# A two-block state space, MLP and gated recurrence kernel: input rows between half weight blocks, decays by a broadcast transfer, output in token halves

## The chip, the cores and the metric

The kernel runs on one core of one Trainium2 chip. The metric is the device time of one execution in microseconds (us). The core has a tensor engine (PE, matmul), a vector engine (DVE), a scalar engine (ACT), GpSimd (POOL) and SyncE (SP), which here only issues transfers. All share one on-chip memory; matmuls accumulate in eight banks of 128 x 512 float32. Transfers run on 16 DMA engines.

## The reference, cut to what matters

Activations are 512 tokens of 1024 channels, float32. Two layers follow each other.

```python
# first layer
u = rmsnorm(x, norm_mix_w)
proj = u @ w_in                       # gate_a, gate_s, b, c, v, z, xbc, dt
y_a = (b * causal_dwconv(c * v, conv_a_w)) @ w_a_out
dt = softplus(dt_raw + dt_bias); a = -exp(a_log)
a_cum = cumsum(dt * a)                # within chunks of 128 tokens
chunk_decay = exp(a_cum[..., -1])     # (4 chunks, 32 heads)
carry = carry * chunk_decay + states  # from chunk to chunk
h = x + (sigmoid(gate_a) * y_a + sigmoid(gate_s) * y_s) @ w_o
h = h + conv_gated_mlp(rmsnorm(h, norm_ffn_w))
h = rmsnorm(h, final_norm_w)
# second layer: gated recurrence (8 heads, both directions) and spatial gating
h = h + merged @ w_out_2
out = rmsnorm(h, final_norm_w_2)
```

## The kernel before

Everything is held transposed, channels on the partitions: `X[128, 8, 512]` is eight rows of 128 channels by 512 tokens. All weights are cut into 285 blocks of 1024 x 128, 512 KB each, in one list `STREAM`. For each block SyncE loads `raw` (ring of four), ACT copies it rounded to `w_high` (ring of three), DVE subtracts to get `w_low`, and PE runs 24 matmuls of 512 columns: for each of eight k `w_high` x high part, `w_high` x low part, `w_low` x high part of the moving activation, all into one bank. The copies of a block are made two blocks ahead of its matmuls (`ahead`). The order on every engine is written out by hand; semaphores tie the engines together (`landed`, `hi_done`, `lo_done`, `block_done`).

The start. SyncE issues the parameters `par`, block 0, X rows 0 to 3 in two transfers, block 1, rows 4 to 7 in two transfers, the constants `cst`, block 2, block 3, and from then on one block for every block done. PE runs four dummy matmuls on `conv_p`, memory set to 1.0. ACT makes `w_high` of block 0, the high part of rows 0 and 1 (`first_row`: X times the norm weight into `early_high`), `w_high` of block 1, rows 2 to 7, block 2, then the squares of all rows (`first_square`). DVE makes the low parts in the same order (`low_row`, `low`), then the sums of squares. The norm's root is applied later, since the first blocks are multiplied before it is known. PE's `pair_blocks` runs blocks 0 and 1 (`conv_c`, `conv_v` of channel block 0) together, with the second `lead=3` steps behind the first; a step's first matmul waits until the row's low part is there (`s_split`). The third block is `conv_b`. Then `stat(0)` sums the squares over the partitions, ACT takes the root, and DVE and ACT make the rows with the root (`u_high`, `u_low`), which PE uses from the seventh block on.

The decays of chunks. After the 25th block (`dt`) DVE and ACT work out `dtw` (32 heads by 512 tokens) and the four decays of each head. DVE multiplies them with an identity (`dsmall[:, 1]`); PE, after the `gate_a` blocks, transposes `dtw` (L608) and multiplies ones with that product (L610), so that every partition has all 128 decays, and DVE copies both out (L1531, L1532). They are used in the state recurrence, `states`. GpSimd's queue writes the running sums to memory and reads them back, one head at a time, to all partitions (`rows_of`, L2072); ACT takes their exponential (L997).

The end. The last block is run in two token halves of 256 (`last_block`): 24 matmuls for each half. `last_stat(half)` sums the squares of a half over the partitions; that of half 0 stands inside half 1's matmuls, ahead of k = 6. ACT takes the root (L1378, L1379). DVE adds the last row (`last_row`, L2047) and scales (L2054) eight rows of half 0, with half 1's `last_row` behind the first, then eight rows of half 1. SyncE stores two rows of all 512 tokens whenever two rows of half 1 are scaled:

```python
for k in range(0, KT, 2):
    sp.wait_ge(s_fin, k + 2)
    sp.dma_start(out.rearrange("(k p) t -> p k t", p=P)[:, k:k + 2], X2[:, k:k + 2]).then_inc(s_out, 16)
```

Of the kernel before, what the change touches and what calls it, by code (L numbers as in the profile page):

```python
# [14 lines left out]
P = 128  # L15
T = 512
# [3 lines left out]
HEADS = 32  # L20
# [210 lines left out]
def build(nc, x_in, wall, par_in, consts_in, masks_in, ws_in, bs_in, spill, running, out):  # L231
    ctx = ExitStack()
    with ctx:
# [29 lines left out]
        identR = fixed("identR", [P, P], F32R)  # L263
# [3 lines left out]
        decay_b = fixed("decay_b", [P, NCH, HEADS], F32)  # L267
# [126 lines left out]
        s_x = [sem(f"s_x{k}") for k in range(KT // 2)]  # L394
# [12 lines left out]
        s_min, s_exp, s_mat, s_y, s_ytaken = (sem(f"ssd_{k}") for k in "min exp mat y ytaken".split())  # L407
        s_rows, s_row = sem("ssd_rows"), [sem(f"ssd_row{k}") for k in range(4)]
# [63 lines left out]
        def _(sp):  # L472
            def load_x(k):
                sp.dma_start(X[:, k:k + 2], x_in.rearrange("(k p) t -> p k t", p=P)[:, k:k + 2]).then_inc(s_x[k // 2], 16)

            sp.dma_start(par[:], par_in).then_inc(s_par, 16)
            for n in range(NBLK):
# [3 lines left out]
                if n == 0:  # L481
                    load_x(0)
                    load_x(2)
                if n == 1:
                    for k in range(4, KT, 2):
                        load_x(k)
                    sp.dma_start(cst[:], consts_in).then_inc(s_cst, 16)
                if n == 2 * RAW_RING:
# [4 lines left out]
            sp.wait_ge(s_out, KT // 2 * 16)  # L493

        @block.tensor
        def _(pe):
# [22 lines left out]
            def pair_blocks(first, second, moving, ready, base, stop=True, between=None, lead=0):  # L519
# [4 lines left out]
                for step in range(KT + lead):  # L524
                    for key, k in ((first, step), (second, step - lead)):
                        if not 0 <= k < KT:
                            continue
# [11 lines left out]
                    if between and step == KT // 2 + 1:  # L539
                        between()  # L540

# [8 lines left out]
            def last_block():  # L550
# [54 lines left out]
            for j in range(3):  # L605
                for c in range(NCH):
                    k = j * NCH + c
                    pe.transpose(side[0][:, k * HEADS:(k + 1) * HEADS], dtw[:, j, c * P:(c + 1) * P],  # L608
                                 cst[0:HEADS, 0, 0:HEADS])
            pe.matmul(side[1][:, 0:NCH * HEADS], cst[0:HEADS, 1], dsmall[:, 1],  # L610
                      start=True, stop=True).then_inc(d_turned, 1)
# [230 lines left out]
        def _(act):  # L842
# [47 lines left out]
            def first_row(k):  # L890
                act.wait_ge(s_x[k // 2], 16)
# [490 lines left out]
        def _(dve):  # L1382
# [62 lines left out]
            dve.wait_ge(s_par, 16)  # L1445
# [31 lines left out]
            for k in range(KT):  # L1477
                mixed_row(k)
                if k in (3, 6):
                    low(5 + (3, 6).index(k))  # L1480
            link(tt(w_both[:], par[:, PCOL["final_norm_w"]:PCOL["final_norm_w"] + KT],
                    par[:, PCOL["norm_w_2"]:PCOL["norm_w_2"] + KT], ALU.mult))
            for j in range(KT):
# [17 lines left out]
                if j == LATE:  # L1501
                    link(cp(identR[:], ident))
# [678 lines left out]
```

## Time and profile before

| | |
|---|---|
| median of 3 runs | 1728.76 us (1727.35 to 1729.48) |
| profiled execution | 1729.27 us |
| its span, first to last instruction | 1727.4 us |
| PE busy | 1707.5 us, 99% of the span |
| PE weight loads (beside the matmuls) | 1401.7 us |
| DVE busy | 1149.6 us, 67% |
| ACT busy | 815.3 us, 47% |
| granted TensorE clock, mean | 0.997 of full |
| moved by the DMA | 174.75 MB, mean 101 GB/s |

All rows come from one profiled execution; its time is 1.87 us more than its span. Times in rows are counted from the span's start. L followed by a number is a line of the kernel; a line can be that of a helper. "Idle before" is how long the engine stood still ahead of an instruction, with what released it.

### The profile page before, as it was taken

The page shows a single profiled execution, that of the slowest core. Times are in us where ns is not written, and L with a number is a line of the kernel's source. Part 1 is how long each engine was busy: PE and PEld are TensorE (multiplying, and loading weights), DVE is VectorE, ACT ScalarE, POOL GpSimd, SP SyncE. Part 2 cuts the span into 40 slices and gives each one's busy share as a digit, 9 for nine tenths or more (in the row PEclk, how much of TensorE's full clock was granted, in tenths as well). Part 3 has the DMA queues.
Part 4 walks back from the last instruction along what each step waited for, and adds up shares of the span by engine and source line. Part 5 has one row for each costly group of instructions (what it writes and reads, how often), then busy time and mean ns, then how long its engine had stood idle before and what let it go on. Part 6 is the DMA issues. An engine that isn't in the chain of part 4 may idle for free.

```text
span 1727.4 us, 22168 instructions
## 1 busy us (share of the span) xinstructions
PE 1707.5 (99%) x8794; PEld 1401.7 (81%) x8794; DVE 1149.6 (67%) x1686; ACT 815.3 (47%) x1162; POOL 29.7 (2%) x55
## 2 busy tenths in 40 slices
PE   8999999999999999999999999999999999999997
PEld 6888888878877888888888888888888888888886
DVE  6844346888886645677775445867768778867664
ACT  5323234755756323322222334667667676665521
POOL 0000000000000000000000000100000000000000
PEclk9999999999999999999999999999999999999999
DMA  4333323333332222223323333722222222222422
GB/s 158 129 98 124 98 98 98 110 105 103 113 107 86 89 96 97 97 98 98 98 98 98 110 101 107 256 86 74 86 74 75 85 74 78 82 86 74 135 96 75
DMA packets 48934, 174.75 MB, mean 101 GB/s; under 512 B 5552, under 2 KB 5680, under 8 KB 48704
## 3 DMA queue, kind: packets, MB, share of 16 engines
q1 hardware_dynamic: 43648, 155.45, 27.4%
q0 software_dynamic: 5184, 17.89, 3.3%
q8 instruction: 70, 1.15, 0.3%
q14 instruction: 32, 0.26, 0.1%
HBM read 164.87 MB, written 4.26 MB: 98 GB/s over the span
## 4 chain that ended last, share of the span: by engine, by line
PE 96%; DVE 2%; ACT 1%; DMA 0%; issue 0%; SPq 0%; DVEq 0%; ACTq 0%
PE bank L513 84%; PE bank L535 2%; PE bank L740 2%; PE bank L668 1%; PE bank L578 1%; PE bank L750 1%; PE bank L666 1%; PE bank L626 1%; PE bank L786 0%; DMA raw<-stream 0%; PE bank L775 0%; PE bank L763 0%; PE bank L647 0%; DVE w_low L1391 0%; DVE X L2054 0%
## 5 line engine op out<-in xcount | busy, mean ns | idle before, releaser
L513 PE MATMUL bank<-u_high,w_high 128*128 128x512 f32 x1568 | 618.4, 394 | 0.0
L513 PE MATMUL bank<-u_high,w_low 128*128 128x512 f32 x1568 | 610.9, 390 | 0.0
L513 PE MATMUL bank<-u_low,w_high 128*128 128x512 f32 x1568 | 610.0, 389 | 0.0
L851 ACT ACTIVATE w_high<-raw 128x1024 fp32r<-128x1024 f32 x285 | 301.0, 1056 | 587.3 <-PE bank L513 579.6
L1391 DVE TENSOR_TENSOR w_low<-raw,w_high 128x1024 fp32r<-128x1024 f32 x285 | 348.2, 1223 | 250.0 <-ACT w_high L851 244.5
L513 PEld LDWEIGHTS bank<-u_high,w_low 128*128 128x128 f32 x1568 | 294.3, 188 | 62.0
L513 PEld LDWEIGHTS bank<-u_high,w_high 128*128 128x128 f32 x1568 | 294.4, 188 | 61.8 <-issue 2.9
L513 PEld LDWEIGHTS bank<-u_low,w_high 128*128 128x128 f32 x1568 | 294.6, 188 | 60.6 <-issue 1.2
L1471 DVE TENSOR_TENSOR h_raw<-bank,rs 128x512 f32<-128x512 f32 x44 | 30.4, 691 | 62.2 <-PE bank L513 55.4
L513 PE MATMUL bank<-f_high,w_high 128*128 128x512 f32 x176 | 68.5, 389 | 0.0
L513 PE MATMUL bank<-f_low,w_high 128*128 128x512 f32 x176 | 68.5, 389 | 0.0
L513 PE MATMUL bank<-f_high,w_low 128*128 128x512 f32 x176 | 68.5, 389 | 0.0
L1833 DVE TENSOR_TENSOR XL<-AG 128x512 f32<-128x512 f32 x80 | 51.6, 686 | 22.8 <-PE bank L740 22.8
L1195 ACT ACTIVATE XL<-XL 128x512 f32<-128x512 f32 x56 | 35.2, 629 | 62.3 <-DVE XL L1833 42.1
L859 ACT ACTIVATE stage<-bank 128x512 f32<-128x512 f32 x24 | 14.3, 595 | 73.5 <-PE bank L513 64.7
L513 PE MATMUL bank<-y_high,w_high 128*128 128x512 f32 x112 | 43.7, 390 | 0.3 <-DVE w_low L1391 0.3
L513 PE MATMUL bank<-y_high,w_low 128*128 128x512 f32 x112 | 43.6, 389 | 0.0
L513 PE MATMUL bank<-y_low,w_high 128*128 128x512 f32 x112 | 43.6, 389 | 0.0
L1851 DVE TENSOR_TENSOR XL<-XL,Q 128x512 f32<-128x512 f32 x56 | 38.3, 688 | 7.4 <-ACT XL L1196 7.1
L1722 DVE TENSOR_TENSOR X<-X,bank 128x512 f32<-128x512 f32 x23 | 15.8, 688 | 35.9 <-PE bank L513 35.7
L513 PEld LDWEIGHTS bank<-f_high,w_high 128*128 128x128 f32 x176 | 33.0, 188 | 6.9
L513 PEld LDWEIGHTS bank<-f_high,w_low 128*128 128x128 f32 x176 | 33.0, 188 | 6.9
(357 smaller groups left out, 2421.9 us busy)
## 6 DMA issues: line engine op xcount, KB each, us to landing
raw<-stream SPq DMA_DIRECT2D x285, 512.0 KB, 3.3
rows<-running POOLq DMA_DIRECT2D x32, 256.0 KB, 3.5
X<-x_t SPq DMA_DIRECT2D x4, 512.0 KB, 7.9
u_high<-n_high_rows POOLq DMA_DIRECT2D x4, 512.0 KB, 5.7
u_low<-n_low_rows POOLq DMA_DIRECT2D x4, 512.0 KB, 6.4
residual<-X POOLq DMA_DIRECT2D x4, 512.0 KB, 8.8
X<-residual POOLq DMA_DIRECT2D x4, 512.0 KB, 5.4
out_t<-X SPq DMA_DIRECT2D x4, 512.0 KB, 3.6
```

Source lines behind the costliest of these rows:

```text
L513: ins = pe.matmul(acc[:], w[:, k], x[:, at + k], start=start and k == first and j == 0, stop=stop and k == KT - 1 and j == 2)
L535: ins = pe.matmul(bank(key)[:], w[:, k], x[:, k], start=k == 0 and j == 0, stop=stop and k == KT - 1 and j == 2)
L578: ins = pe.transpose(side[2][:, n * P:(n + 1) * P], src[:, c * P:(c + 1) * P], ident)
L626: ins = pe.transpose(bank3[:, c * P:(c + 1) * P], src[:, c * P:(c + 1) * P], ident)
L666: ins = pe.matmul(y[rows, cs], xdec[:, c - 1, hs], cexp[h % 4][:, cs], start=False, stop=True)
L740: ins = pe.matmul(side[at % 2][half * e:half * e + half, to], XL[:, at % 3, 0, keys], XL[:, at % 3, 1, to], start=True, stop=True)
L851: act.activation(w_high[:, n % HI_RING], raw[:, n % RAW_RING], ACT.Copy).then_inc(hi_done, 1)
L1195: act.activation(x[:, 0], x[:, 0], ACT.Exp, scale=1.0 if n == 0 else -1.0)
L1391: tt(w_low[:, n % RAW_RING], raw[:, n % RAW_RING], w_high[:, n % HI_RING].bitcast(F32), ALU.subtract).then_inc(lo_done, 1)
L1471: give(tt(out, bank(key)[:], rs[:], ALU.mult), key)
L1833: ins = tt(two(x, first, step, w), a, b, ALU.subtract)
L1851: tt(x, x, Q[:, h % 2], ALU.mult).then_inc(x_pair, 1)
```

## The change

Start: X comes in eight transfers of one row, and blocks 0 and 1 come in two halves of four k each. The order is half block 0, the first eight columns of the parameters, row 0, half block 1, rows 1 to 3, second half 0, row 4, second half 1, rows 5 to 7, block 2, constants, the other parameters, block 3. ACT and DVE make `w_high` and `w_low` of these blocks by halves. PE runs three dummies instead of four, and a new `first_blocks` runs both blocks side by side, k by k; its first matmul of a row waits for the row's high part alone, the second for the low part. `pair_blocks` loses `lead`, which only this place used.

Middle: the decays are written by GpSimd's queue to memory and read back to all partitions. DVE's product, PE's matmul and DVE's copy go, and so does an unused rounded copy of the identity. `decay_b` is laid out heads by chunks.

End: `last_stat(0)` stands ahead of k = 4. `last_row(1)` stands behind the fourth scaling of half 0. Each scaling counts `s_fin`. Half 0 is stored in two transfers of four rows, half 1 in four transfers of two rows, each of 256 tokens.

```diff
@@ sync
+            def load_half(n, half):
+                ks = slice(half * KT // 2, (half + 1) * KT // 2)
+                sp.dma_start(raw[:, n, ks], wall[n].rearrange("p (k c) -> p k c", k=KT)[:, ks]).then_inc(
+                    landed[n] if half else half_landed[n], 16)
+
+            first_columns = PCOL["norm_mix_w"] + KT
+            load_half(0, 0)
+            sp.dma_start(par[:, 0:first_columns], par_in[:, 0:first_columns]).then_inc(s_norm, 16)
+            load_x(0)
+            load_half(1, 0)
+            for k in range(1, 4):
+                load_x(k)
+            load_half(0, 1)
+            load_x(4)
+            load_half(1, 1)
+            for k in range(5, KT):
+                load_x(k)
+            for n in range(2, NBLK):
...
-            for k in range(0, KT, 2):
-                sp.wait_ge(s_fin, k + 2)
-                sp.dma_start(out.rearrange("(k p) t -> p k t", p=P)[:, k:k + 2], X2[:, k:k + 2]).then_inc(s_out, 16)
+            for half, rows in enumerate((4, 2)):
+                ts_ = slice(half * T // 2, half * T // 2 + T // 2)
+                for k in range(0, KT, rows):
+                    sp.wait_ge(s_fin, half * KT + k + rows)
+                    sp.dma_start(out.rearrange("(k p) t -> p k t", p=P)[:, k:k + rows, ts_], X2[:, k:k + rows, ts_]).then_inc(s_out, 16)
@@ tensor
+            def first_blocks():
+
+                for k in range(KT):
+                    for n in range(2):
+                        if n == 0:
+                            pe.wait_ge(n_high, k + 1)
+                        if k == 0:
+                            pe.wait_ge(hi_half, n + 1)
+                        elif k == KT // 2:
+                            pe.wait_ge(hi_done, n + 1)
+                        pe.matmul(ps[n][:], w_high[:, n, k], early_high[:, k], start=k == 0, stop=False)
+                        if n == 0:
+                            pe.wait_ge(s_split, k + 1)
+                        pe.matmul(ps[n][:], w_high[:, n, k], early_low[:, k], start=False, stop=False)
+                        if k == 0:
+                            pe.wait_ge(lo_half, n + 1)
+                        elif k == KT // 2:
+                            pe.wait_ge(lo_done, n + 1)
+                        ins = pe.matmul(ps[n][:], w_low[:, n, k], early_high[:, k], start=False, stop=k == KT - 1)
...
-                        if half and k == KT - 2:
+                        if half and k == KT // 2:
                             last_stat(0)
...
-            for _ in range(4):
+            for _ in range(3):
                 pe.matmul(side[1][:], conv_p[:, 0:P], conv_p[:], start=True, stop=True)
-            pair_blocks(("conv_c", 0), ("conv_v", 0), EARLY_ROWS, s_split, KT * EARLY, lead=3)
+            first_blocks()
...
-            pe.matmul(side[1][:, 0:NCH * HEADS], cst[0:HEADS, 1], dsmall[:, 1],
-                      start=True, stop=True).then_inc(d_turned, 1)
+            ins.then_inc(d_turned, 1)
@@ scalar
-            high(0)
-            act.wait_ge(s_par, 16)
-            for k in range(2):
+            high_half(0, 0)
+            act.wait_ge(s_norm, 16)
+            first_row(0)
+            high_half(1, 0)
+            for k in range(1, 4):
                 first_row(k)
-            high(1)
-            for k in range(2, KT):
+            high_half(0, 1)
+            first_row(4)
+            high_half(1, 1)
+            for k in range(5, KT):
                 first_row(k)
@@ vector
-            low(0)
+            low_half(0, 0)
+            dve.wait_ge(s_norm, 16)
             for k in range(KT):
                 low_row(EARLY, k, pcol("norm_mix_w", k), *first)
-                if k == 1:
-                    low(1)
+                if k == 0:
+                    low_half(1, 0)
+                if k == 3:
+                    low_half(0, 1)
+                if k == 4:
+                    low_half(1, 1)
...
+            dve.wait_ge(s_par, 16)
...
-                    link(cp(identR[:], ident))
...
-            cp(decay_b[:].rearrange("p c h -> p (c h)"), side[1][:, 0:NCH * HEADS]).then_inc(d_tok, 1)
+            cp(tok[:].rearrange("p a c h -> p (a c h)"), side[0][:, 0:3 * NCH * HEADS]).then_inc(d_tok, 1)
...
+            dve.wait_ge(s_decay, 32)
...
-                    if half == 0 and k == 0:
+                    stt(X2[:, k, ts_], X2[:, k, ts_], pcol("final_norm_w_2", k), rs[:, ts_], ALU.mult, ALU.mult).then_inc(s_fin, 1)
+                    if half == 0 and k == 3:
                         last_row(1, side[2])
@@ gpsimd
+            pool.wait_ge(d_exp, 2)
+            pool.dma_start(decays, dsmall[:, 0, 4:8]).then_inc(s_decay, 16)
             pool.wait_ge(s_rows, 16)
+            pool.wait_ge(s_decay, 16)
+            pool.dma_start(decay_b[:].rearrange("p h c -> p (h c)"),
+                           bass.AP(decays.tensor, decays.offset, [[0, P], [1, NCH * HEADS]])).then_inc(s_decay, 16)
```

## Rows read from the trace of the kernel before

**Rows 1.** From the page: busy time of PE, with its share of the span.
```profile
PE 1707.5 (99%) x8794; PEld 1401.7 (81%) x8794; DVE 1149.6 (67%) x1686; ACT 815.3 (47%) x1162; POOL 29.7 (2%) x55
```

**Rows 2.** The chain that ended last, 0 to 60 us: start, us, what.
```profile
2.64 7.90 DMA raw<-stream
...
13.60 11.43 PE bank L535 x42
25.03 5.44 PE bank L513 x24
```

**Rows 3.** Windows of the start: busy (x), PEclk, DMA share, GB/s.
```profile
0.00:4.00 4.00, 2.04 (x3) 1.01 (x4) 0.72 (x5) 1.28 (x1) 0.20 (x4) 1.00 0.56 174
4.00:5.00 1.00, 1.00 (x3) 0.48 (x2) 0.00 (x0) 0.39 (x1) 0.00 (x0) 1.00 0.76 150
5.00:8.00 3.00, 3.00 (x5) 0.88 (x4) 1.22 (x1) 0.67 (x1) 0.00 (x0) 1.00 1.00 321
8.00:13.00 5.00, 1.75 (x7) 1.00 (x6) 2.76 (x4) 3.77 (x6) 0.00 (x0) 1.00 1.04 409
8.10:9.60 1.50, 0.00 (x0) 0.00 (x0) 0.79 (x2) 1.29 (x2) 0.00 (x0) 1.00 1.03 404
11.30:13.60 2.30, 0.00 (x1) 0.01 (x1) 1.95 (x3) 2.30 (x5) 0.00 (x0) 1.00 1.06 424
13.60:17.10 3.50, 3.50 (x9) 2.72 (x10) 3.50 (x6) 3.50 (x6) 0.00 (x0) 0.52 0.41 166
```

**Rows 4.** Timeline of PE, 0 to 9 us: the dummies.
```profile
1.96 6.14 PE L591 MATMUL bank<-conv_p 128*128 128x512 f32 x8 [1.96 <-DVE conv_p L1418]
```

**Rows 5.** Line L474, the X transfers: issue ns and starts, landing.
```profile
L474 SPq DMA_DIRECT2D X<-x_t x4: 427/494/1430, 1.7 to 3.7; - x4
...
DMA to landing us min/median/max: 6.3/7.9/9.3
```

**Rows 6.** Groups by line and shape, 0 to 31 us: busy us, mean ns.
```profile
L1391 DVE TENSOR_TENSOR w_low<-raw,w_high 128x1024 fp32r<-128x1024 f32 x5 | 6.1, 1225 | 7.8 <-ACT w_high L851 7.8
L1428 DVE SCALAR_TENSOR_TENSOR early_low<-X,par,early_high 128x512 fp32r<-128x512 f32 x8 | 5.5, 748 | 1.8 <-ACT early_high L874 1.8
L851 ACT ACTIVATE w_high<-raw 128x1024 fp32r<-128x1024 f32 x5 | 5.3, 1053 | 3.8 <-DMA raw<-stream 3.8
L874 ACT ACTIVATE early_high<-X,par 128x512 fp32r<-128x512 f32 x8 | 5.1, 708 | 2.4 <-DMA X<-x_t 2.4
L888 ACT ACTIVATE sq_first<-X 128x512 f32<-128x512 f32 x8 | 4.3, 614 | 0.0
L1454 DVE TENSOR_TENSOR sums<-sums,sq_first 128x512 f32<-128x512 f32 x6 | 4.2, 692 | 0.2
```

**Rows 7.** Timeline of DVE, 45 to 47 us.
```profile
45.35 1.47 DVE L1423 TENSOR_TENSOR u_low<-scaled,u_high 128x512 fp32r<-128x512 f32 x2
```

**Rows 8.** The chain, 190 to 200 us.
```profile
195.43 0.30 PE bank L610 x2
```

**Rows 9.** Transfers by line: KB each, median us from issue to landing.
```profile
rows<-running POOLq DMA_DIRECT2D x32, 256.0 KB, 3.5
```

**Rows 10.** Line L997, the exponentials of rows: ns, first and last start.
```profile
L997 ACT ACTIVATE cexp<-rows x32: 613/617/633, 294.1 to 539.9; 128x512 f32<-128x512 f32 x32
```

**Rows 11.** The chain, from 1690 us to the end.
```profile
1708.98 5.03 PE bank L562 x42
...
1715.88 0.48 DVE X L2054
...
1719.07 0.40 DVEq L233
1719.46 3.17 DVE X L2054 x8
```

**Rows 12.** Timeline of ACT, 1717 to 1728 us.
```profile
1718.44 0.42 ACT L1379 ACTIVATE rs<-rs 128x256 f32<-128x256 f32 x1
```

**Rows 13.** Line L492, the stores: from issue to landing.
```profile
DMA to landing us min/median/max: 2.8/3.6/4.3
```

More of the change, by code:

```diff
@@ L228, with build @@
 TILE = tiles()
-def build(nc, x_in, wall, par_in, consts_in, masks_in, ws_in, bs_in, spill, running, out):
+def build(nc, x_in, wall, par_in, consts_in, masks_in, ws_in, bs_in, spill, running, decays, out):
     ctx = ExitStack()
@@ L262, in build @@
         ident, ones, upper = cst[:, 0], cst[:, 1], cst[:, 2]
-        identR = fixed("identR", [P, P], F32R)
         masks = fixed("masks", [P, len(LEVELS), T], U8)
@@ L266, in build @@
         tok = fixed("tok", [P, 3, NCH, HEADS], F32)
-        decay_b = fixed("decay_b", [P, NCH, HEADS], F32)
+        decay_b = fixed("decay_b", [P, HEADS, NCH], F32)
         acum_at = base[0]
@@ L393, in build @@
         s_par, s_cst, s_masks, s_out = sem("s_par"), sem("s_cst"), sem("s_masks"), sem("s_out")
-        s_x = [sem(f"s_x{k}") for k in range(KT // 2)]
+        s_x = [sem(f"s_x{k}") for k in range(KT)]
+        s_norm = sem("s_norm")
+        half_landed, hi_half, lo_half = [sem(f"half_landed{s}") for s in range(2)], sem("hi_half"), sem("lo_half")
         vstep, astep = sem("vstep"), sem("astep")
@@ L517, in wblock, with pair_blocks @@
                     ins.then_inc(block_done, 1)
-            def pair_blocks(first, second, moving, ready, base, stop=True, between=None, lead=0):
+            def pair_blocks(first, second, moving, ready, base, stop=True, between=None):
                 for key in (first, second):
@@ L523, in pair_blocks @@
                 xh, xl = moving
[L524 to L527, printed above, removed]
+                for k in range(KT):
+                    for key in (first, second):
                         n = AT[key]
@@ L538, in pair_blocks @@
                             ins.then_inc(block_done, 1)
-                    if between and step == KT // 2 + 1:
+                    if between and k == KT // 2 + 1:
                         between()
+            def first_blocks():
+                for k in range(KT):
+                    for n in range(2):
[14 more added lines that the diff above has]
+                        ins = pe.matmul(ps[n][:], w_low[:, n, k], early_high[:, k], start=False, stop=k == KT - 1)
+                        if k == KT - 1:
+                            ins.then_inc(block_done, 1)
             def stat(n, both=False):
@@ L890, in first_row, with high_half @@
             def first_row(k):
-                act.wait_ge(s_x[k // 2], 16)
+                act.wait_ge(s_x[k], 16)
                 high_row(k, pcol("norm_mix_w", k), early_high)
-            high(0)
-            act.wait_ge(s_par, 16)
-            for k in range(2):
+            def high_half(n, half):
+                ks = slice(half * KT // 2, (half + 1) * KT // 2)
+                act.wait_ge(landed[n] if half else half_landed[n], 16)
+                act.activation(w_high[:, n, ks], raw[:, n, ks], ACT.Copy).then_inc(hi_done if half else hi_half, 1)
+            high_half(0, 0)
[3 more added lines that the diff above has]
+            for k in range(1, 4):
                 first_row(k)
-            high(1)
-            for k in range(2, KT):
+            high_half(0, 1)
+            first_row(4)
+            high_half(1, 1)
+            for k in range(5, KT):
                 first_row(k)
@@ L1444, in _, with low_half @@
             first = (early_high, early_low)
-            dve.wait_ge(s_par, 16)
-            low(0)
+            def low_half(n, half):
+                ks = slice(half * KT // 2, (half + 1) * KT // 2)
+                dve.wait_ge(hi_done if half else hi_half, n + 1)
+                tt(w_low[:, n, ks], raw[:, n, ks], w_high[:, n, ks].bitcast(F32),
+                   ALU.subtract).then_inc(lo_done if half else lo_half, 1)
+            low_half(0, 0)
+            dve.wait_ge(s_norm, 16)
             for k in range(KT):
                 low_row(EARLY, k, pcol("norm_mix_w", k), *first)
-                if k == 1:
-                    low(1)
+                if k == 0:
[4 more added lines that the diff above has]
+                    low_half(1, 1)
             low(2)
@@ L2177 @@
     running = nc.dram_tensor("running", (HEADS, T), F32, kind="Internal").ap()
-    build(nc, *args, spill, running, out)
+    decays = nc.dram_tensor("decays", (HEADS, NCH), F32, kind="Internal").ap()
+    build(nc, *args, spill, running, decays, out)
     r = run_bass_kernel_spmd(nc, [arrays], core_ids=[0])
```

28 lines of the change are left out of this document (8 added, 20 removed).

## The prediction, made before the kernel was changed

> **What bounds the kernel now.** I read the busy times first: TensorE (PE) is busy in 1707.5 us of a span of 1727.4 [rows 1]. It sets the time, and VectorE (DVE), ScalarE (ACT) and the DMA matter only where PE stands still for them. In steady work a 512-column matmul starts every 0.227 us (a block of 24 takes 5.44 us [rows 2]; its own row says 0.39 us because two overlap). The change touches no matmul of that body, so I read the two ends and one spot in the middle.
>
> The chain that ended last, over the first 60 us, shows the start [rows 2]: nearly 8 us of waiting for the second weight block, then DVE, then from 13.60 to 25.03 the matmuls of the first two blocks. The 48 matmuls of those blocks need 48 x 0.227 = 10.9 us; they begin at 9.6 but the third block begins at 25.03. Where the difference went is in the windows [rows 3]. Dummy matmuls on `conv_p` fill PE from 1.96 for 6.14 us [rows 4]. Then a stop of 1.5 us, six real ones, a stop of 2.3 us, and 3.5 us at a mean granted clock of 0.52, that is at 1.2 GHz. After the first stop the clock had stayed at 2.4 GHz [rows 3].
>
> The cause of the stop is the loading order. By the windows the DMA has moved 0.70 MB at 4 us, 0.85 at 5, 1.81 at 8, and 409 GB/s from there [rows 3]. The first X transfer lands at 1.7 + 6.3 = 8.0 us, the last at 3.7 + 9.3 = 13.0 [rows 5], the second weight block at 2.64 + 7.90 = 10.5 [rows 2]. Queued up to then are 1.22, 3.32 and 2.27 MB (params 0.17, each other transfer 0.52). So a transfer in the busy stretch lands once about 0.55 MB more than its own end has moved (0.58, 0.51, 0.58). This is my clock for the new order.
>
> **The start, step by step.** The same bytes come in a new order, in pieces of 0.26 MB: half block 0, row 0, half block 1, rows 1 to 3, second half 0, row 4, second half 1, rows 5 to 7, then block 2, consts, the rest of the parameters, block 3. Putting 0.55 MB on each sum and reading the moved bytes gives these landings: the first half block ahead of row 0; row 0 by 5.7, or from about 4.2 if the first transfers meet less queue; half block 1 at 6.5; rows 1 to 3 at 7.4, 8.1, 8.8; second half 0 at 9.4; row 4 at 10.1; second half 1 at 10.7; rows 5 to 7 at 11.3, 12.0, 12.6; block 2 at 13.9. SyncE issues 13 transfers ahead of block 2 instead of 7; at the 0.49 us of the median issue [rows 5] row 7 is issued at 6.6 us, before its bytes' turn, so the issue is hidden behind the transfers. One issue before took 1.43 us [rows 5]; if all did, the thirteenth would go out at 18 us, an end for the range.
>
> ACT per row 0.63 to 0.71 us, DVE 0.68 to 0.75 [rows 6]; a half block costs ACT 0.61 (the 512-wide squares) and DVE 0.69 (the 512-wide sums) [rows 6], so the four halves cost 2.8 us on DVE against 2.4 for two wholes, hidden while DVE keeps ahead of PE. The new `first_blocks` starts with the high part of the row and no longer waits for the low one.
> - Three dummies instead of four: one is two of the eight records, 1.7 us, so PE is free at 8.1 - 1.7 = 6.4 [rows 4]. Row 0 is ready by then. The first real matmul starts at 6.4, not 9.6.
> - Half block 1: ACT 6.6 to 7.2, DVE to 7.95. PE finishes k = 0 of both blocks about 8.2, with small stops.
> - Row 1: ACT 7.4 to 8.1, DVE 8.15 to 8.9. Its first matmul runs at 8.3, the next at 8.95, and five more matmuls end k = 1 at 10.1.
> - From there a k costs 6 x 0.227 = 1.36 us, while DVE delivers rows 2 to 7 at 9.6, 10.3, 11.7, 13.1, 13.8, 14.5 (second half 0 at 11.0 and second half 1 at 12.4 lie between). PE wants them at 10.1, 11.4, 12.8, 14.2, 15.5, 16.9. Rows are ahead from k = 2 on: PE bound, 10.1 + 6 x 1.36 = 18.25 us. (The chain counts a matmul from the end of the record before it, 0.39 - 0.227 = 0.16 us after its own start, so it will say 18.4 where it says 25.03 now.)
>
> The third block then starts at 18.4 instead of 25.03: **6.6 us less**. For this the next things must not be late. Block 2: landed 13.9, ACT 1.05, DVE 1.22 [rows 6]: 16.2, 2 us ahead. ACT's eight squares follow to 19.2, DVE's sums to 21.3; `stat(0)` wants them at 18.25 + 5.44 = 23.7. Block 3: ACT 20.8, DVE 22.5, wanted at 24.5. All after it hangs on `stat(0)` and moves with it; the closest point there is DVE's last split of u_low, done at 46.8 [rows 7]; PE reaches its blocks 3 x 5.44 us after `stat(0)`, not before 46.8, and both move alike.
>
> Bounds. Best: PE never stops after 6.4, 6.4 + 10.9 = 17.3, a gain of 7.6. Worst that I hold likely: everything lands 1.5 us later (gain 5.1), or a slow stretch of the clock falls on these matmuls (3.4 us at half speed, 1.7 us lost, gain 4.9), or both (3.4).
>
> One rule of the Trainium skill speaks against this start. TensorE: Matmul & The Clock Gate, "What's actually happening", has the engine throttled by default, until it was busy, and again after idling. The trace disagrees on the first half: the granted clock is 1.00 from the first dummy on [rows 3]. On the second half it agrees, as the stretch after the 2.3 us stop shows. By the rule a shorter run of dummies and stops after 6.4 would risk the 1.7 us above (rival A). By the rows, a stop of 1.5 us cost no clock, and the new start has none as long.
>
> **The middle.** The broadcast of the chunk decays by a matmul goes: two records, 0.30 us on the chain [rows 8], at a place where PE had nothing else: **0.3 us less** (0 to 0.5). On DVE two copies (identity, decays) and a small product go, beside PE. In their place GpSimd's queue writes 128 numbers and reads them back to all partitions, with a wait for the exponentials. The nearest row is the 3.5 us of a row broadcast, four times its size [rows 9]; two of them in series and two issues are some 8 us more ahead of the first row's broadcast. What is queued behind it there are the rows, and the first exponential of one is at 294 us [rows 10], while this code follows the 25th block, which ends near 25.03 + 23 x 5.44 = 150 us. More than 100 us of cover; without it, it would cost 8 us once. The strided read of `decay_b` keeps 512 outputs: 0. Moved addresses (constants, masks, tok, sums) and smaller ring orders for the later pair of blocks: 0, same instructions.
>
> **The tail.** `last_stat(0)` comes two k earlier, 6 matmuls of 5.03 / 42 = 0.12 us [rows 11]: the first half's root is 0.72 earlier, and DVE starts its scalings at 1715.16, not 1715.88. Four of them, not one, now stand ahead of `last_row(1)`: on before's time axis it starts at 1715.16 + 4 x 0.40 = 1716.75, where it came at 1716.28, one scaling after 1715.88 (+0.47). From there to the second root nothing changes: 1718.86 + 0.47 = 1719.33 (Exp starts 1718.44, takes 0.42 [rows 12]). DVE has done the first half at 1718.8 and waits; the eight scalings of 3.17 us [rows 11] end at 1722.5, against 1722.63: 0.1 less. The 0.40 us of DVE's queue between the halves [rows 11] lies in the wait.
>
> Then the stores. Before, four of 512 KB leave in 2.4 us, and the last lands 4.3 us after its issue [rows 13]: 2.1 MB at the 409 GB/s of the start take 5.1 us, longer than DVE needs to make them, so they queue. Now half of the bytes leave earlier, and the four late stores have 0.26 MB each, 0.64 us of data at that rate every 0.79 us: no queue. The first store before, alone, landed in 2.8 us [rows 13]; less 0.64 that is 2.2. I take 2.4, as rows of 1 KB instead of 2 KB have no row of their own here. Last landing 1725.0 instead of 1727.0: with DVE's 0.1 **2.0 us less**. Bounds: 2.3 less; or, if 1 KB rows cost as much as 2 KB rows each, the second early store and four late ones need 2.6 + 4 x 1.3 us from 1719.7, ending about 1 us later than before.
>
> **Sum.** The profiled execution took 1729.27 us, 1.87 around its span. 6.6 + 0.3 + 2.0 = 8.9 less gives 1720.4. It was 0.5 above the median of the runs, 1728.76, so against that: **1719.9**.
>
> **The rivals.**
> - A: a slow stretch of the clock in the first blocks. For: it happened, after too little work. Against: PE works nearly without stop from 6.4. 1719.9 + 1.7 = 1721.6.
> - B: the pieces land about 2 us later than my clock says, by issues or by doubled 2 KB pieces. For: the irregular first microseconds (150 GB/s from 4 to 5). PE waits that long at k = 1: 1721.9.
> - C: the 1 KB rows of the stores take the tail's 2.0 and 1 more: 1722.9.
> - D: small transfers stream at half the rate, 200 GB/s. The stream starts near 2.3 us (0.70 MB at 4), so block 2, with 3.67 + 0.55 MB, lands at 2.3 + 21.1 = 23.4 and its split is done at 25.7, 0.8 after the third block started before; less the 2.3 of middle and tail: 1727.3, within 0.2% of before. Against: the X transfers had 2 KB pieces as well and ran at 409 GB/s among others, so D and E get small chances.
> - E, slower: the stream stays at the 150 GB/s of the window from 4 to 5 us [rows 3]. Block 2 lands at 2.3 + 28.1 = 30.4, is split at 32.7, and the third block starts 7.8 later than before; less 2.3, 5.5 us slower: 1734.3. It decides from a rate below about 190 GB/s.
>
> The Trainium skill, DMA: Bandwidth & Descriptors, "Measured", asks for transfers of at least 1 MiB and gives about 2.0 us fixed plus bytes at 436 GB/s. Taken one by one, 256 KB would need 2.6 us, as an estimate 101 GB/s, and would make D or E out of the halving; the trace's queue overlaps them (409 GB/s with 512 KB transfers).
>
> **Numbers.** Forecast 0.62, A 0.13, B 0.12, C 0.05, D 0.05, E 0.03. The runs of the kernel before lie within 1.4 us of their median. Low end: 7.6 + 0.5 + 2.3 = 10.4 less, 1718.4, and 0.8 for that scatter: 1717.6. High end: 3.4 + 0 + 1.6 = 5.0 less: 1723.8, which holds A, B and C. 0.2% is 3.5 us, about what this measurement tells from nothing. Faster by more: all but D and E, 0.91; same 0.06; slower 0.03.
>
> **What would show it.** In the profile after: third block starting near 18.4 us; first real matmul near 6.4; granted clock 1.00 throughout the first 20 us; rows landing about every 0.65 us from 7.4; no matmul after the transposes of the middle; the last store landing 2.4 us after its issue; DVE's last scaling ending near 1722.6 - 7.0 = 1715.6. It is wrong if PE waits for rows from k = 2 on, if the clock falls, or if a wait on sums or block 3 appears after 18 us.

## The result and the profile after

The changed kernel takes 1719.52 us (median of 5 runs, 1719.27 to 1719.82) against 1729.48 for the kernel before, run beside it (5 runs, 1727.35 to 1729.61): a ratio of 0.9947, 95% interval 0.9935 to 0.9958. The prediction said 1719.9, range 1717.6 to 1723.8. The profiled execution took 1719.67 us, its span is 1717.8 against 1727.4: 9.6 us less. The trace says where.

Busy time, from the page of the changed kernel. PE works 3.5 us less than in [rows 1], the rest of the 9.6 us was standing still or storing:

```profile
PE 1704.0 (99%) x8790; PEld 1399.9 (81%) x8790; DVE 1149.3 (67%) x1685; ACT 816.0 (48%) x1164; POOL 30.6 (2%) x57
```

The chain that ended last of the changed kernel, 0 to 60 us (start, us, what). L629 are the dummies, L568 a first matmul of a row, L531 the third block on:

```profile
1.96 4.78 PE bank L629 x6
6.74 0.23 PE bank L568
...
17.93 5.44 PE bank L531 x24
23.36 0.86 PE bank L584 x2
```

There is no DMA in it any more, and no DVE behind the dummies. (The weight load of the second matmul, at 6.89, still waits for row 0's low part; from 6.90 on the row of matmuls is unbroken.) The third block starts at 17.93 where [rows 2] has 25.03: **7.1 us less**, 6.6 forecast.

The transfers of X rows in the changed kernel (issue ns and starts, then issue to landing), to be held against [rows 5]:

```profile
L477 SPq DMA_DIRECT2D X<-x_t x8: 424/432/568, 1.7 to 6.4; - x8
...
DMA to landing us min/median/max: 3.5/4.7/5.9
```

Row 0 lands at 1.66 + 3.5 = 5.2, row 7 at 6.44 + 5.9 = 12.3. The windows of the start (columns as in [rows 3]) show one stream without the dip at 4 us:

```profile
0.00:4.00 4.00, 2.04 (x3) 1.01 (x4) 0.72 (x5) 1.67 (x2) 0.20 (x4) 1.00 0.52 118
4.00:5.00 1.00, 1.00 (x3) 0.48 (x2) 0.69 (x1) 0.25 (x1) 0.00 (x0) 1.00 0.88 283
5.00:8.00 3.00, 3.00 (x9) 1.47 (x9) 1.84 (x3) 2.49 (x5) 0.00 (x0) 1.00 1.01 357
8.00:13.00 5.00, 5.00 (x23) 3.98 (x22) 4.81 (x8) 4.63 (x8) 0.00 (x0) 1.00 1.03 386
```

From 5 us on PE is busy in the whole of every stretch (3.00 of 3.00, 5.00 of 5.00), where before it worked 1.75 of the 5 us from 8 to 13. The transfers are no faster for it: in the first 4 us they move 118 GB/s instead of 174, and at 8 us both kernels have moved 1.8 MB. What changed is which bytes come first.

The chain in the middle, 186 to 200 us. The transposes are followed at once by the next block; the 0.30 us of [rows 8] are gone: **0.3 us less**, as forecast:

```profile
187.47 0.86 PE bank L646 x12
188.33 11.78 PE bank L531 x51
```

The chain at the end, from 1680 us (L600 the half matmuls, L1424 and L1425 the root on ACT, L2108 the scalings, L2101 the last row):

```profile
1701.54 4.31 PE bank L600 x36
...
1707.72 1.67 DVE X L2108 x4
1709.39 0.34 DVE X L2101
...
1711.47 0.42 ACT rs L1425
...
1711.92 0.49 DVE X L2108
1712.40 0.39 DVEq L233
1712.80 2.38 DVE X L2108 x6
```

From the first half matmul to the last scaling it is 1715.18 - 1701.54 = 13.64 us; before, 1722.63 - 1708.98 = 13.65 [rows 11]. DVE won nothing. The stores did (line L510):

```profile
L510 SPq DMA_DIRECT2D out_t<-X x6: 372/372/408, 1709.4 to 1715.2; - x6
...
DMA to landing us min/median/max: 2.1/2.2/2.9
```

The two of 512 KB land 2.9 us after their issue, the four of 256 KB 2.1 to 2.2, the last one 2.2; before the last took 4.3 [rows 13]. From the first half matmul to the end of the span: 16.26 us now, 18.42 before, **2.2 us less**. 7.1 + 0.3 + 2.2 = 9.6, the whole difference of the spans.

### The profile page after: what moved, and what is told of

Its sections match the earlier page's. It is cut to its first block, busy times and chain, and to the rows that moved or that the text cites. A ratio compares the mean times of both kernels' runs of the same rounds, so it can differ in the third digit from the quotient of the medians.

```text
span 1717.8 us, 22175 instructions
## 1 busy us (share of the span) xinstructions
PE 1704.0 (99%) x8790; PEld 1399.9 (81%) x8790; DVE 1149.3 (67%) x1685; ACT 816.0 (48%) x1164; POOL 30.6 (2%) x57
## 4 chain that ended last, share of the span: by engine, by line
PE 97%; DVE 2%; ACT 1%; issue 0%; DVEq 0%; ACTq 0%
PE bank L531 85%; PE bank L777 2%; PE bank L551 2%; PE bank L705 1%; PE bank L616 1%; PE bank L787 1%; PE bank L703 1%; PE bank L663 1%; PE bank L823 0%; PE bank L812 0%; PE bank L800 0%; PE bank L684 0%; PE bank L814 0%; PE bank L816 0%; DVE w_low L1437 0%
## 5 line engine op out<-in xcount | busy, mean ns | idle before, releaser
L531 PE MATMUL bank<-u_high,w_high 128*128 128x512 f32 x1568 | 618.5, 394 | 0.0
L531 PE MATMUL bank<-u_high,w_low 128*128 128x512 f32 x1568 | 610.9, 390 | 0.0
L531 PE MATMUL bank<-u_low,w_high 128*128 128x512 f32 x1568 | 610.0, 389 | 0.0
L531 PEld LDWEIGHTS bank<-u_high,w_low 128*128 128x128 f32 x1568 | 294.3, 188 | 62.0
L531 PEld LDWEIGHTS bank<-u_high,w_high 128*128 128x128 f32 x1568 | 294.4, 188 | 61.8 <-issue 2.9
L531 PEld LDWEIGHTS bank<-u_low,w_high 128*128 128x128 f32 x1568 | 294.6, 188 | 60.5 <-issue 1.2
L531 PE MATMUL bank<-f_high,w_high 128*128 128x512 f32 x176 | 68.5, 389 | 0.0
L531 PE MATMUL bank<-f_low,w_high 128*128 128x512 f32 x176 | 68.5, 389 | 0.0
L531 PE MATMUL bank<-f_high,w_low 128*128 128x512 f32 x176 | 68.5, 389 | 0.0
L531 PE MATMUL bank<-y_high,w_high 128*128 128x512 f32 x112 | 43.7, 390 | 0.3 <-DVE w_low L1437 0.3
L531 PE MATMUL bank<-y_high,w_low 128*128 128x512 f32 x112 | 43.6, 389 | 0.0
L531 PE MATMUL bank<-y_low,w_high 128*128 128x512 f32 x112 | 43.6, 389 | 0.0
L531 PEld LDWEIGHTS bank<-f_high,w_high 128*128 128x128 f32 x176 | 33.0, 188 | 6.9
L531 PEld LDWEIGHTS bank<-f_high,w_low 128*128 128x128 f32 x176 | 33.0, 188 | 6.9
```

The source lines that it names most:

```text
L531: ins = pe.matmul(acc[:], w[:, k], x[:, at + k], start=start and k == first and j == 0, stop=stop and k == KT - 1 and j == 2)
```

## The experiments

Twelve kernels ran, in three groups: 1 to 4, 5 to 8 and 9 to 12, each group beside the kernel before on one chip. Medians are compared with the kernel before of the same group (1728.59, 1727.9, 1727.9 us); places of the chain come from one profiled execution each.

**1. The end undone.** The changed kernel with the old stores, sum and last row:

```diff
-            for half, rows in enumerate((4, 2)):
...
+            for k in range(0, KT, 2):
+                sp.wait_ge(s_fin, k + 2)
+                sp.dma_start(out.rearrange("(k p) t -> p k t", p=P)[:, k:k + 2], X2[:, k:k + 2]).then_inc(s_out, 16)
...
-                        if half and k == KT // 2:
+                        if half and k == KT - 2:
```

> The changed kernel with the end of the kernel before (stores of two rows by 512 tokens, the half sum ahead of k = 6, the last row behind the first scaling). Theory: start and middle give 7.4 us, the end 2.2, all of it from the stores. So the span is 1717.8 + 2.2 = 1720.0 and the last store lands about 4.3 us after its issue, DVE's last scaling near 1715.2. Rival: the earlier bytes were hidden anyway and the start gave more than it seems: less than 1 us lost.

Median 1722.49 us (ratio 0.9963, 0.995 to 0.9976), span 1720.2. From the first half matmul at 1701.84 to the end of the span 18.36 us, 2.1 more than in the changed kernel. Line L508 of this kernel, the stores:

```profile
L508 SPq DMA_DIRECT2D out_t<-X x4: 372/398/546, 1713.1 to 1715.5; - x4
...
DMA to landing us min/median/max: 2.8/3.6/4.3
```

The last scaling ends at 1715.49, and the three landings are those of [rows 13] to the digit: the queue of late stores is back, and the whole price with it. The rival falls. The span is 0.2 above the forecast, since the third block started at 18.26 here.

**2. The end alone**, on the kernel before (the same edits the other way):

```diff
+            for half, rows in enumerate((4, 2)):
+                ts_ = slice(half * T // 2, half * T // 2 + T // 2)
...
```

> The kernel before with only the new end. Theory: 2.2 us less than before, a span of 1725.2; the granted clock still falls to half for about 3.4 us near 13.6 and the third block still starts at 25.0. Rival: the end depends on nothing at the start, but the stores' 1 KB rows cost more than they give: 0 to 1 us less.

Ratio 0.9987 (0.9977 to 0.9996), about 2.2 us under the kernel before. One of its ten runs took 7574.08 us, at a mean granted clock of 0.215; nothing on record says why. The ratio leaves it out, and the other nine have a median of 1726.07. Span 1725.0. Third block at 24.94, the first half matmul at 1708.77, from there 16.23 us. Its chain and the landings of its stores:

```profile
13.50 11.44 PE bank L537 x42
24.94 5.44 PE bank L515 x24
```

```profile
L494 SPq DMA_DIRECT2D out_t<-X x6: 372/372/399, 1716.6 to 1722.4; - x6
...
DMA to landing us min/median/max: 2.1/2.2/2.9
```

Shown from both sides: the end is worth 2.1 to 2.2 us, whatever the start is. The slow stretch of the clock came here too, but later: PE stood for 2.48 and for 2.30 us, the matmuls behind the second stop still started 0.23 us apart until 15.0, and from there to 18.4 us 0.43 apart.

**3. Which part of the end.** The stores kept, the sum and the last row put back:

```diff
-                        if half and k == KT // 2:
+                        if half and k == KT - 2:
                             last_stat(0)
...
-                    if half == 0 and k == 3:
+                    if half == 0 and k == 0:
```

> The changed kernel, stores included, with the half sum back ahead of k = 6 and the last row back behind the first scaling. Theory: DVE's order decides nothing, its last scaling ends within 0.1 us of 1715.2, span 1717.8 to 1717.9. Rival: the earlier sum is part of the end's gain: 0.7 us slower, span 1718.5.

Median 1720.4 (0.9954, 0.9937 to 0.997). The span is 1718.3, nearer to the rival's 1718.5 than to the theory's 1717.9, but mostly for another reason: the third block started at 18.26, 0.3 later, by a start that has the same code. From the first half matmul (1701.84) to the last scaling (1715.49) it is 13.65 us, as in both other kernels; to the end of the span 16.46, 0.2 more than in the changed kernel, since the first early store is now issued at 1710.8 and the late ones queue a little. These two orders on DVE end alike; all but 0.2 us of the end's gain is the stores'.

**4. The stop filled**, on the kernel before:

```diff
                         n = AT[key]
+                        if key == first and lead and k == 2:
+                            pe.matmul(side[1][:], conv_p[:, 0:P], conv_p[:], start=True, stop=True)
                         if key == first:
                             pe.wait_ge(ready, base + k + 1)
```

> The kernel before with one more dummy product in PE's stop near 11 us, ahead of the third k. Theory: the slow stretch of the clock follows the stop; filled, the 42 matmuls from 13.5 run at full clock, 9.5 us instead of 11.4, and the third block starts at 23.1: 1.9 us less, a span of 1725.5. Rival: the clock falls all the same, since the dummy ends at about 12.7 and a stop remains: no change, span 1727.4.

Median 1727.97 against 1728.59, ratio 0.9995 (0.9986 to 1.0004): not told from no change. Neither theory described its profile. Windows and chain:

```profile
6.85:10.27 3.42, 1.36 (x4) 0.47 (x3) 1.54 (x3) 1.33 (x2) 0.00 (x0) 0.96 1.03 381
10.27:13.70 3.43, 3.43 (x8) 2.20 (x8) 1.99 (x3) 2.75 (x4) 0.00 (x0) 0.54 1.05 420
```

```profile
12.92 1.17 PE bank L530 x2
14.09 9.71 PE bank L537 x42
23.80 5.44 PE bank L513 x24
```

The clock fell here too, but near 10 us, after the first stop of 2.06 us ahead of the first row, so it lay on the six early matmuls and on the dummy; the 42 matmuls ran at 2.4 GHz, 9.71 us instead of 11.43, and the third block started 1.2 earlier. The slow stretch is real; on the 42 matmuls it cost 1.7 us (11.43 against 9.71), but which matmuls it hits differs between executions. The length of the stop just ahead does not decide it by itself: here the clock fell behind a stop of 2.06 us, in experiment 2 not behind one of 2.48. Whether the filling would keep the clock when it falls late is not shown.

**5. and 6. Four dummies, and none**, in the changed kernel:

```diff
-            for _ in range(3):
+            for _ in range(4):
```

> The changed kernel with four dummy products instead of three. Theory: once it has begun, PE sets the pace, so a later beginning is paid at the end of the two blocks: start near 7.9 instead of 6.2 with no stops after, third block at 18.9 in the chain instead of 17.9: 1.0 us slower, span 1718.8. Rival: the rows set the pace, and the dummy is hidden: 0.

> The changed kernel with no dummy product. Theory (the trace of before, granted clock 1.00 at the first dummy): the clock is full at the start of the program, the first matmul still waits for row 0 at 6.0, and nothing changes by more than 0.2 us. Rival (the Trainium skill, TensorE: Matmul & The Clock Gate, has the engine throttled until it was busy): the first matmuls run at 1.2 GHz for about 3.4 us and the third block starts 1.7 us or more later: span 1719.5 or above.

Four: median 1720.51, third block at 18.69, first matmul at 7.20. None: median 1720.72, third block at 18.98, though its first matmul began at 5.37. The timeline of PE without dummies:

```profile
6.77 0.63 PE L576 MATMUL bank<-early_high,w_low 128*128 128x512 f32 x1
7.20 0.69 PE L568 MATMUL bank<-early_high,w_high 128*128 128x512 f32 x1
...
9.82 0.55 PE L568 MATMUL bank<-early_high,w_high 128*128 128x512 f32 x1
10.21 0.39 PE L571 MATMUL bank<-early_low,w_high 128*128 128x512 f32 x1
10.43 0.39 PE L576 MATMUL bank<-early_high,w_low 128*128 128x512 f32 x1
```

Until about 10 us the matmuls start 0.43 us apart, then 0.227: half the rate, 1.2 GHz, after the start of the program. The window of the same kernel still prints a granted clock of 1.00:

```profile
6.85:10.27 3.42, 3.42 (x10) 2.45 (x9) 2.58 (x4) 2.74 (x5) 0.00 (x0) 1.00 1.00 321
```

So ahead of the first change on record that number was no measurement, and the spacing is. The kernel before says the same, in the weight loads of its dummies:

```profile
5.53 0.34 PEld L591 LDWEIGHTS bank<-conv_p 128*128 128x128 f32 x1 [0.52 <-issue]
6.39 0.34 PEld L591 LDWEIGHTS bank<-conv_p 128*128 128x128 f32 x1 [0.52 <-issue]
7.08 0.19 PEld L591 LDWEIGHTS bank<-conv_p 128*128 128x128 f32 x1 [0.36 <-issue]
```

0.86 us from record to record is twice the 0.43 that the same kind of product takes in `stat(0)` (0.86 for two records). The dummies run at 1.2 GHz until about 7 us. In experiment 2, the same code, they do so only until about 4.9:

```profile
4.68 0.25 PEld L593 LDWEIGHTS bank<-conv_p 128*128 128x128 f32 x1 [0.52 <-issue]
5.17 0.19 PEld L593 LDWEIGHTS bank<-conv_p 128*128 128x128 f32 x1 [0.24 <-issue]
```

That is what TensorE: Matmul & The Clock Gate ("What's actually happening") of the Trainium skill states, throttled by default; the traces agree. The theory for no dummies falls, its rival stands in direction, with 1.05 us at most (18.98 against 17.93) instead of 1.7 or more, the first matmuls having had to wait for rows in part anyway. By the profile the dummies earn their place. A fourth one moved the first matmul by 0.7 to 1.0 us and the third block by some 0.5 (how far either is outside the scatter, experiment 9 says).

**7. Rows in pairs.** X in four transfers again, in the new order:

```diff
-                sp.dma_start(X[:, k:k + 1], x_in...[:, k:k + 1]).then_inc(s_x[k], 16)
+                if k % 2 == 0:
+                    sp.dma_start(X[:, k:k + 2], x_in...[:, k:k + 2]).then_inc(s_x[k], 16)
```

> The changed kernel with X in four transfers of two rows, in the same places of the order as rows 0, 2, 4 and 6 (so rows 0 and 1 come ahead of half block 1). Theory: a transfer lands a transfer's size later than its bytes, so row 0 lands near 6.9 instead of 5.2; first matmul near 7.6, third block near 18.9: 1.0 us slower, span 1718.8. Rival: the size of the pieces does not matter, PE makes up for it: within 0.2 us.

Median 1720.34, third block at 18.74, near the forecast place of 18.9, though the first pair landed at 1.66 + 4.3 = 6.0 and not 6.9; the first matmul was at 6.87. So the place came out and the theory behind it, a landing one transfer's size behind its bytes, did not: at 6.0 the stream had moved 1.16 MB, 0.37 more than was queued up to that pair, not 0.52.

**8. The second block three k behind**, as it was:

```diff
-                for k in range(KT):
-                    for n in range(2):
+                for step in range(KT + 3):
+                    for n, k in ((0, step), (1, step - 3)):
+                        if not 0 <= k < KT:
+                            continue
```

> The changed kernel with the second block three k behind the first, as before, all loads and waits kept. Theory: PE has only three matmuls for each early row and waits for rows; 0.5 us slower, third block near 18.4, span 1718.3, clock full. Rival 1: those waits are long enough for a slow stretch of the clock, 2 us or more slower. Rival 2: the order of the matmuls is worth nothing once the rows come in time: 0.

Median 1720.79, no slow stretch. The chain's third block:

```profile
19.01 5.44 PE bank L531 x24
```

PE began at 6.24, as early as in the changed kernel, and then stood between 7.3 and 9.4 for rows 1 and 2: its matmuls start at 7.60, 8.39, 8.73, 8.96 and 9.38. With both blocks side by side there are six matmuls for each row instead of three. The loss is 0.3 to 1.1 us against the six profiles of experiment 9, up to twice the forecast. That is the smaller part of the mechanism: with the old order of the matmuls the new loads alone bring the third block from 25.03 to 19.01, 6.0 us, and work for both blocks on each row adds 0.3 to 1.1.

**9. The changed kernel again**, as a measure of all this:

> The changed kernel itself, unchanged, beside the three others on the same chip. The first matmuls start between 6.1 and 6.5 us and the third block between 17.9 and 18.3, depending on when the clock rises under the dummies (0.86 us between their records before, 0.43 after): span 1717.8 to 1718.2.

Median 1720.15 against 1727.9 (0.9954, 0.9942 to 0.9967). Its third block started at 18.68, outside what I expected. The chain of its start, and its X rows:

```profile
2.58 4.88 DMA X<-x_t
...
8.24 0.77 DVE early_low L1474
...
9.05 0.50 PE bank L571
...
18.68 5.44 PE bank L531 x24
```

```profile
L477 SPq DMA_DIRECT2D X<-x_t x8: 424/432/548, 1.6 to 6.4; - x8
...
DMA to landing us min/median/max: 3.7/5.4/6.6
```

The median row landed 0.7 us later than in the first profile, with the same code and order; from 8 to 9 us the DMA moved 291 GB/s, not 356. Row 1 landed at 2.58 + 4.88 = 7.46, and PE waited for its low part until 9.05. Six profiles with this start have the third block at 17.93, 18.00, 18.14, 18.26, 18.26 and 18.68. Two things move it. In the two at 18.26 (experiments 1 and 3) nothing stopped PE behind its second matmul, but that came only at 7.41 instead of 6.90, behind dummies that ran at 1.2 GHz to their end. In the one at 18.68 the dummies were as slow (second matmul at 7.46), and row 1 was late besides. So experiments 5 and 7 (18.69, 18.74) lie at the edge of that scatter and are only likely; 6 and 8 (18.98, 19.01) and the next (19.13) lie outside it, with one profile each. The medians do not tell any of them from the changed kernel: the ratios of 5 to 8 are 0.9955 to 0.9959, each with an interval that holds 0.9954.

**10. Row 0 ahead of half block 0**, with two dummies:

```diff
-            load_half(0, 0)
             sp.dma_start(par[:, 0:first_columns], par_in[:, 0:first_columns]).then_inc(s_norm, 16)
             load_x(0)
+            load_half(0, 0)
...
-            for _ in range(3):
+            for _ in range(2):
```

> The changed kernel with the first parameters and row 0 issued and converted ahead of half block 0, and two dummies. Theory: row 0 and the half block are ready 0.4 us sooner, the first matmul starts near 5.7, but k = 1 waits for row 1 at 7.4 and 8.2 as before: the third block at most 0.2 us earlier. Rival 1: PE's start sets all, 0.45 us earlier. Rival 2: with one dummy less the clock rises later or falls again, 0.3 to 1.7 us slower.

ACT and DVE convert in the same order. Median 1720.05 (0.9955, 0.9943 to 0.9968), the same as the changed kernel. In the profile the first matmul is at 5.79, near the forecast 5.7, but the third block at 19.13, 0.5 to 1.2 later. After three matmuls PE stands until 8.02, for half block 1, which landed 5.2 us after its issue (3.7 in the changed kernel). The windows show the dip that the kernel before had in [rows 3]:

```profile
4.00:5.00 1.00, 1.00 (x3) 0.16 (x1) 0.24 (x1) 0.66 (x1) 0.00 (x0) 1.00 1.15 162
5.00:6.00 1.00, 0.95 (x2) 0.24 (x2) 0.84 (x2) 0.63 (x1) 0.00 (x0) 1.00 0.64 219
```

None of the three theories named this: the stream of the first microseconds is itself uneven. Why, is open.

**11. The last row earlier**, and **12. with the last store cut in two**:

```diff
-                    if half == 0 and k == 3:
+                    if half == 0 and k == 1:
                         last_row(1, side[2])
...
+                pieces = [(k, rows) for k in range(0, KT, rows)] if half == 0 else [(0, 2), (2, 2), (4, 2), (6, 1), (7, 1)]
```

> The changed kernel with the last row of half 1 behind the second scaling instead of the fourth. Theory: DVE stops before the second half, since the second root comes 0.6 us after its eighth scaling; the root is 0.8 earlier and DVE goes on without a stop, so its last scaling and the last landing are 0.5 to 0.6 us earlier: span 1717.2. Rival: PE's half sums or ACT are late instead (half 1's matmuls end 0.3 us before), and less than 0.2 us is won.

> The changed kernel with the last row behind the second scaling and the last store of two rows cut into two of one row (0.13 MB). Theory: 0.5 to 0.6 from DVE as in the kernel before it, and half of the last store's 0.64 us of data, 0.3: 0.9 us less than the changed kernel, the last store landing 1.9 us after its issue. Rival: the time from issue to landing of a lone store is nearly all latency, so the cut gives under 0.1.

11: median 1719.55 (0.9954, 0.994 to 0.9968), span 1717.4. Chain at the end and stores:

```profile
1701.57 4.31 PE bank L600 x36
...
1708.95 2.37 DVE X L2108 x6
1711.33 0.40 DVEq L233
1711.72 2.77 DVE X L2108 x7
```

```profile
L510 SPq DMA_DIRECT2D out_t<-X x6: 372/373/407, 1709.8 to 1714.5; - x6
...
DMA to landing us min/median/max: 2.4/2.7/3.0
```

DVE no longer waits between the halves: 12.92 us from the first half matmul to the last scaling instead of 13.64, 0.7 less. The stores give 0.3 of it back, as they follow each other more closely (median landing 2.7 instead of 2.2). To the end of the span 15.83 us instead of 16.26 and 16.23 in the two profiles of the changed kernel: 0.4 less, shown in the profile. The medians (1719.55 against 1720.15) point the same way, but their runs overlap.

12: median 1719.82 (0.9953, 0.994 to 0.9965), span 1717.5, 15.79 us from the first half matmul. The last store, half as large, landed 2.2 us after its issue, against 2.4 for the whole one of experiment 11, but it was issued later, behind the other half: 0.04 us is left for the cut. The rival is right in the sum; of the 2.4 us, halving the bytes took 0.2. Experiments 11 and 12 are the best versions and not told apart; they beat the changed kernel by 0.4 us in the profile and by less than the runs can tell.

## Why the prediction was right, step by step

**The bound.** PE, but for the two ends and one spot. The body between the third block and the last one shrank by 0.34 us, of which the two records of the middle are 0.30. Right.

**The start, 6.6 forecast, 7.1 measured (6.35 to 7.1 in the six profiles).** That PE is the bound once k = 2 has begun is shown by its matmuls: the first of k = 2 starts at 9.58 in the first profile and at 10.34 in experiment 9, and 36 matmuls of 0.227 us lead from there to 17.75 and 18.51, just where the third block starts (17.93 and 18.68 in the chain, which counts 0.16 later). The step "PE free at 6.4, first matmul then" came out (6.17 and 6.46), but partly by luck. I took 1.7 us for a dummy product at a clock that was full from the first dummy. That is its price at 1.2 GHz, two records 0.86 us apart; the dummies ran so for most of the time, and for how long varies. A dummy more, at the end of the row where the clock has risen, moved the first matmul by only 0.7 to 1.0 us (experiment 5). The sentence that weighed the rule of the Trainium skill against the trace has it the wrong way round, as experiment 6 showed: its "disagrees on the first half" rested on the printed clock of 1.00.

The landing clock, 0.55 MB beyond a transfer's own end, was too slow for the first profile. Its row 7, the last of 3.15 MB, landed at 12.35, when about 3.5 MB had moved: 0.35 MB beyond. Rows 1 to 3 landed at 6.7, 7.3 and 8.0 instead of 7.4, 8.1 and 8.8, so k = 1 ended at 9.58 and not at 10.1: this is the term that made 6.6 of 7.1. In experiment 9, with the same code, rows 1 to 3 landed at 7.5, 8.1 and 8.8, as the clock said, 0.45 to 0.57 MB beyond their own ends, and the start gave 6.35. So the lag is no constant, and not the size of a transfer either; what sets it is open. The forecast of 6.6 lies inside what the same start does from one execution to the next.

Rival A, the slow stretch on the first blocks, did not come in any of the six profiles. B, pieces 2 us later than my clock, did not come either; in experiment 9 they came as the clock said, 0.7 us later than in the first profile. D and E did not come: the stream ran at 357 to 386 GB/s with 256 KB transfers. Which of the new parts gave the 6.0 us that experiment 8 leaves to the loads (rows between the blocks, blocks in halves, the first matmul of a row not waiting for the low part) no run separates; experiment 7 puts single rows against pairs at 0.06 to 0.8 us. Two slips change nothing in the sum: eight transfers, not seven, stood ahead of block 2 before, and the chances of all but D and E add up to 0.92, not 0.91.

**The middle, 0.3 forecast, 0.3 measured.** GpSimd's queue wrote the decays at 151.8 us, issued their broadcast at 154.7 and the first row at 155.3; the first exponential came at 286.7, about 130 us later. The cover was as large as stated. No run undoes the middle alone, but the body shows it: 1683.56 to 1683.62 us from the third block to the first half matmul in the eleven profiles with the new middle, 1683.83 to 1683.95 in the three with the old one.

**The tail, 2.0 forecast, 2.2 measured.** The second root came 0.47 us later relative to the half matmuls, as worked out, and DVE's last scaling 0.0 earlier instead of 0.1. I misread one row: "DVEq L233 0.40" in [rows 11] is no wait but one of the sixteen scalings, which the chain writes by its queue; the counts 1 + 6 + 8 need it. Half 0 ended at 1719.46 before, directly followed by half 1. The conclusion that DVE now waits was right, and experiment 11 took that wait away. The stores' 2.4 us from issue to landing was 2.2; rival C, dear 1 KB rows, did not come.

**The base.** I subtracted from an execution of 1729.27 us. The kernel before scatters from 1726.55 to 1729.62 over all groups, the changed one from 1719.27 to 1720.43. In the result the gain is 10.0 us, in experiment 9, the only other pair, 7.8; that 8.9 lies between them, and 1719.9 within 0.4 of the median, owes something to which executions were drawn. The clock goes with the scatter: of the 20 runs of the kernel before beside experiments 1 to 4, the six with a mean granted clock of 0.998 took 1727.19 to 1727.93 us, the fourteen with 0.996 or 0.997 took 1728.27 to 1729.62. Half speed for 3.4 us is 0.001 of this mean and 1.7 us of time, an estimate from [rows 3] that fits. Experiment 4 shows one way to it, the slow stretch ahead of the 42 matmuls, 1.2 us less in the chain; that the faster runs had no such stretch, or had it where PE stood anyway, is argued, since no profile of one was taken.

## What to carry to other kernels

At the start of this program the time to the first unbroken row of matmuls was set first by the order of the loads (6.0 us) and then by how much work each arriving piece gives (up to 1.1). Cut the first weights and activations so that the first products need little, and run side by side all that a piece serves. At the end, let the bytes leave as they are ready: a lone last store of 256 KB took 2.2 us from issue to landing, behind a queue it took two more. And read a clock off the spacing of like instructions before trusting a printed one.

## What the runs showed of the hardware that I had not expected

- The granted clock printed for a stretch ahead of the first recorded change was 1.00 while matmuls of 512 columns started 0.43 us apart, at 1.2 GHz. The change to 0.227 us came between 4.9 and 7 us under dummies and near 10 us without.
- How far a landing lagged behind the bytes moved was not fixed by the size of the transfer: 0.54 to 0.59 MB with 512 KB pieces in the kernel before, 0.2 to 0.43 with 512 KB rows in experiment 7, 0.2 to 0.35 with 256 KB ones in the first profile of the changed kernel, 0.36 to 0.57 in its second.
- In the first 6 us the stream can dip: 150 GB/s from 4 to 5 us in the kernel before, 162 and 219 from 4 to 6 in experiment 10, 283 and more in the two profiles of the changed kernel. What decides it was not found.
- Halving a last store from 256 to 128 KB changed its time from issue to landing by 0.2 us (2.4 to 2.2).
- The clock did not fall at once behind a stop: in experiment 2 the matmuls behind a stop of 2.30 us, from 13.5 to 15.0 us, ran 0.23 us apart, and those from 15.4 to 18.4 us 0.43 apart.
